# Early expert tiles with 512-column matmuls, their halves added on VectorE, their weight splits made on GpSimd

## The chip, the cores and the metric

One core of one Trainium2 chip runs the whole program. The metric is device time in microseconds (us): the median of the runs, lower is better. Engines: TensorE (PE; its weight loads are listed as PEld), VectorE (DVE), ScalarE (ACT), GpSimd (POOL) and SyncE (SP), which issues the DMAs.

## The reference

Two layers over 256 tokens of width 1024. Each layer has a mixer part (a combined input projection, three kinds of attention, gates, an output projection) and a PEER part, where the change lies:

```python
def peer_ffn(h, w_query, q_norm_peer, sub_keys_1, sub_keys_2, expert_u, expert_v):
    qr = rms_norm((h @ w_query).reshape(bsz, seq, PEER_HEADS, PEER_DKEY), q_norm_peer)
    s1 = jnp.einsum('bshd,hnd->bshn', qr[..., :half], sub_keys_1)
    s2 = jnp.einsum('bshd,hnd->bshn', qr[..., half:], sub_keys_2)
    v1, i1 = lax.top_k(s1, PEER_TOPK)
    v2, i2 = lax.top_k(s2, PEER_TOPK)
    ...
    top_s, top_pos = lax.top_k(cand_s, PEER_TOPK)
    idx = jnp.take_along_axis(cand_i, top_pos, axis=-1)
    g = jax.nn.softmax(top_s, axis=-1)
    ...
        u = jnp.take(expert_u, ix, axis=0)
        act = jax.nn.gelu(jnp.einsum('td,ted->te', hx, u))
        vv = jnp.take(expert_v, ix, axis=0)
        return jnp.einsum('te,ted->td', (gx * act), vv)
```

The kernel does not gather. It computes gelu(u . h) for all 16384 experts (128 tiles of 128 experts), multiplies by the routing weights, which are zero for experts not chosen, and multiplies by all of expert_v.

## The kernel before, in words

Weights come as a stream of tiles of 128x1024 fp32 through four raw buffers. ScalarE rounds each tile to fp32r (`head`, output `hi`, L496), and VectorE makes the rest raw - hi (`rest_of`, output `lo`, L873). Activations are kept in the same way as `mov_hi` and `mov_lo`, in 12 slots of 256 columns. A product is three matmuls: high weights by high activations, high weights by low activations, low weights by high activations (`product`, L1453 to L1455). A tile has 8 chunks (KC) of 128 rows, so an "up" tile is 24 matmuls of 256 columns into one of two PSUM banks `pj`. `hi` and `lo` have four buffers each (SPLIT): the head of tile t+3 waits until tile t-1 is done.

The 128 up tiles of a layer fall in two groups. The first 96 (EARLY) run while VectorE finds the top 16 keys of 8 heads for two blocks of tokens and turns positions into expert indices (the picks, L1315 to L1326). ScalarE applies gelu straight from the bank (`early_group`, L757) and frees the bank. VectorE's splits of these tiles are placed by hand between the top-k instructions (`split_early`). After tile 80 (EXP_AT) ScalarE changes its function table to take the softmax's exponents; after tile 84 (ROUTE_AT) TensorE transposes the indices and weights, and VectorE copies them (`route_in`). Then come 32 mixed tiles (STEPS): in each, TensorE also multiplies one-hot rows of 8 tokens (`tokens`, L1814), made by VectorE (`onehot_a`, L1351), by GpSimd (even groups of four tokens, `quad`, L484) and by ScalarE (odd ones, L788 and L792). The one-hots of GpSimd and ScalarE lie in slots 8 to 11 of `mov_hi` and `mov_lo`. Last come 128 down tiles with 512-column matmuls into `wk`.

Each engine runs its own program in order. Semaphores: `hi_done`, `lo_done` (splits made), `tile_done` (tile multiplied), `out_free` (bank read out), `hot_b` (one-hots made), `hot_used`. In the text tile 0 is the first early tile, tile 96 the first mixed one.

Of the kernel before, what the change touches and what calls it, by code (L numbers as in the profile page):

```python
# [20 lines left out]
P = 128  # L21
# [90 lines left out]
def trunk(nc, stream, par_dram, const_dram, mix_dram, taba_dram, keys_dram, front_dram, ada_dram, x_dram, out_dram):  # L112
# [4 lines left out]
    with ctx:  # L117
# [11 lines left out]
        mov_hi = sb("mov_hi", [P, 12, SEQ], f32r)  # L129
        mov_lo = sb("mov_lo", [P, 12, SEQ], f32r)  # L130
        w_hi = mov_hi[:, KC:KC + 4, :]
        w_lo = mov_lo[:, KC:KC + 4, :]
# [13 lines left out]
        onehot_b = [w.rearrange("p a b -> p (a b)").rearrange("p (r i) -> p r i", r=8) for w in (w_hi, w_lo)]  # L146
# [185 lines left out]
        route_in = sem("route_in")  # L332
        hot_a = sem("hot_a")
# [115 lines left out]
        def _(pool):  # L449
            for l in range(DEPTH):  # L450
# [39 lines left out]
        def _(act):  # L490
# [45 lines left out]
            for l in range(DEPTH):  # L536
# [324 lines left out]
        def _(dve):  # L861
# [80 lines left out]
            for l in range(DEPTH):  # L942
# [293 lines left out]
                early = [0]  # L1236

                def split_early(n):
                    for _ in range(min(n, EARLY - early[0])):
                        j = early[0]  # L1240
                        rest_of(L0 + (T_PEER + AHEAD + j), j + AHEAD)
                        early[0] += 1

                split_early(1)
# [9 lines left out]
                for u in range(17):  # L1254
# [15 lines left out]
                    split_early(1)  # L1270
# [6 lines left out]
                    split_early(1)  # L1277
# [4 lines left out]
                    split_early(u % 2)  # L1282
# [8 lines left out]
                    split_early(1)  # L1291
# [18 lines left out]
                split_early(1)  # L1310
                for n in range(2):
                    for b in range(2):
                        hot = pick.rearrange("p (c j) -> p c j", j=16)
                        pf = pos_f[:, n, b * 128:(b + 1) * 128]
                        one_hots = step(nc.vector.tensor_tensor(  # L1315
                            hot, pf.unsqueeze(2).to_broadcast([P, 128, 16]),
                            iota[:, 0:16].unsqueeze(1).to_broadcast([P, 128, 16]), ALU.is_equal))
                        split_early(2 if n + b else 1)
                        dve.wait_ge(dve_step, one_hots)
                        hot4 = pick.rearrange("p (u k j) -> p u k j", u=8, k=16)  # L1320
                        picked = step(nc.vector.tensor_tensor(
                            hot4, hot4, sel_if[:, b * 8:b * 8 + 8, n, :].unsqueeze(2).to_broadcast([P, 8, 16, 16]),
                            ALU.mult))
                        split_early(1)
                        dve.wait_ge(dve_step, picked)
                        link(nc.vector.tensor_reduce(idx_tok[:, n, b * 128:(b + 1) * 128], hot, AX.X, ALU.add))  # L1326
                        split_early(2 if n and b else 1)
                assert early[0] <= EXP_AT
                split_early(EXP_AT - early[0])
# [3 lines left out]
                split_early(1)  # L1333
# [5 lines left out]
                split_early(ROUTE_AT - early[0])  # L1339
# [110 lines left out]
        def _(pe):  # L1450
# [28 lines left out]
            for l in range(DEPTH):  # L1479
# [299 lines left out]

                def early_tile(j, between=None):  # L1780

                    project(L0 + (T_PEER + j), j, O_PEER + j, (j + 1) % 2, None if j else M_2, between=between,
                            between_at=KC - 1).then_inc(tile_done, 1)
# [5 lines left out]
                with pe.Fori(1, ROUTE_AT // 4) as i:  # L1789
                    for j in range(4):  # L1790
                        project(L0 + i * 4 + (T_PEER + j), j, i * 4 + (O_PEER + j), (j + 1) % 2).then_inc(tile_done, 1)
# [7 lines left out]
                for j in range(EARLY - ROUTE_AT):  # L1799
                    project(L0 + (T_PEER + ROUTE_AT + j), j, O_PEER + ROUTE_AT + j, (j + 1) % 2).then_inc(tile_done, 1)  # L1800
# [177 lines left out]
```

## Time and profile before

| | us |
|---|---|
| median of 3 runs | 2183.56 (2183.55 to 2184.15) |
| profiled execution, its span | 2181.1 |
| early tiles of the first layer | about 327 to 603 |
| mixed tiles of the first layer | about 603 to 752 |
| down tiles of the first layer | about 752 to 1097 |
| the same three in the second layer | about 1401 to 2171 |

The span runs from the first to the last instruction of the profiled execution. What is outside of it, and the difference between this execution and the median, make 2.5 us together. Busy times of the matmul rows overlap each other (a matmul is recorded as 283 ns while the next starts 120 ns later), so the rate has to be read from starts or from counts in a stretch.

### The profile page before, as it was taken

What the parts mean: (1) busy time and instruction counts of PE and PEld (TensorE: products, weight loads), DVE (VectorE), ACT (ScalarE), POOL (GpSimd) and SP (SyncE); (2) the same over time, 40 slices, a digit from 0 to 9 for tenths busy, and PEclk for the clock granted to TensorE, in tenths of its full rate; (3) what the DMA queues carried; (4) which work ended last, traced back from release to release, by engine and by line L of the source; (5) the groups of instructions that cost most, each with busy time, mean ns of one, the idle gap of its engine ahead of it and who ended that gap; (6) DMA issues with size and microseconds to landing.
All of it is one profiled execution on the core that took longest, in us unless ns stands there. A gap on an engine that the chain in (4) does not pass through costs nothing.

```text
span 2181.1 us, 43026 instructions
## 1 busy us (share of the span) xinstructions
PE 2151.9 (99%) x15008; PEld 1989.8 (91%) x15008; DVE 1680.4 (77%) x3258; ACT 1233.9 (57%) x2168; POOL 245.7 (11%) x298
## 2 busy tenths in 40 slices
PE   6999999999999999999999999999999999999999
PEld 5889999999999988888888899999999999888887
DVE  8777777889499956777577878788886997567765
ACT  5656575444577655555566565644455776555554
POOL 0210000000166400000002100000002662000000
PEclk8999999999999999999999999999999999999999
DMA  9466655555533367787665666455555334687864
GB/s 352 156 223 229 204 188 173 182 182 182 184 122 110 125 193 260 258 253 231 192 202 176 221 231 206 162 183 183 179 177 175 115 116 144 200 272 258 254 211 171
DMA packets 115440, 427.29 MB, mean 196 GB/s; under 512 B 12816, under 2 KB 13072, under 8 KB 113680
## 3 DMA queue, kind: packets, MB, share of 16 engines
q1 hardware_dynamic: 115344, 426.08, 58.2%
q8 instruction: 51, 0.84, 0.2%
q14 instruction: 45, 0.37, 0.0%
HBM read 424.99 MB, written 1.05 MB: 195 GB/s over the span
## 4 chain that ended last, share of the span: by engine, by line
PE 96%; DVE 2%; ACT 1%; DMA 1%; issue 0%; SPq 0%; ACTq 0%; DVEq 0%
PE pj L1453 18%; PE pj L1455 18%; PE pj L1454 18%; PE wk L1453 11%; PE wk L1455 11%; PE wk L1454 11%; PE wk L1814 5%; PE wk L1583 1%; PE wk L1560 1%; DMA arena<-in_front 1%; PE wk L1576 1%; PE wk L1522 1%; DVE arena L878 0%; PE wk L1743 0%; ACT hi L496 0%
## 5 line engine op out<-in xcount | busy, mean ns | idle before, releaser
L873 DVE TENSOR_TENSOR lo<-raw,hi 128x1024 fp32r<-128x1024 f32 x683 | 843.3, 1236 | 417.7 <-ACT hi L496 412.1
L496 ACT ACTIVATE hi<-raw 128x1024 fp32r<-128x1024 f32 x683 | 721.4, 1057 | 470.9 <-PE wk L1455 341.5
L1453 PE MATMUL pj<-mov_hi,hi 128*128 128x256 f32 x3008 | 867.8, 288 | 1.8 <-DVE x L1204 1.3
L1455 PE MATMUL pj<-mov_hi,lo 128*128 128x256 f32 x3008 | 851.5, 283 | 0.0
L1454 PE MATMUL pj<-mov_lo,hi 128*128 128x256 f32 x3008 | 850.9, 283 | 0.0
L1453 PEld LDWEIGHTS pj<-mov_hi,hi 128*128 128x128 f32 x3008 | 577.0, 192 | 10.9 <-issue 8.3
L1454 PEld LDWEIGHTS pj<-mov_lo,hi 128*128 128x128 f32 x3008 | 576.5, 192 | 0.1
L1455 PEld LDWEIGHTS pj<-mov_hi,lo 128*128 128x128 f32 x3008 | 575.9, 191 | 0.0
L1453 PE MATMUL wk<-hi,mov_hi 128*128 128x512 f32 x1024 | 398.5, 389 | 0.0
L1454 PE MATMUL wk<-lo,mov_hi 128*128 128x512 f32 x1024 | 398.4, 389 | 0.0
L1455 PE MATMUL wk<-hi,mov_lo 128*128 128x512 f32 x1024 | 398.4, 389 | 0.0
L484 POOL TENSOR_SCALAR mov_hi<-const,routes 128x128 fp32r<-128x128 f32 x256 | 199.4, 795 | 1012.8 <-DVE gateT L1343 866.7
L757 ACT ACTIVATE arena<-pj 128x256 f32 (+1 forms) x192 | 73.9, 385 | 275.4 <-PE pj L1455 275.4
L1455 PEld LDWEIGHTS wk<-hi,mov_lo 128*128 128x128 f32 x1024 | 192.2, 188 | 40.1
L1454 PEld LDWEIGHTS wk<-lo,mov_hi 128*128 128x128 f32 x1024 | 192.2, 188 | 39.9
L1453 PEld LDWEIGHTS wk<-hi,mov_hi 128*128 128x128 f32 x1024 | 192.2, 188 | 39.6
L1351 DVE TENSOR_SCALAR onehot_a<-const,routes,gateT 128x128 f32<-128x128 f32 x512 | 148.4, 352 | 2.2 <-PE wk L1814 2.2
L878 DVE SCALAR_TENSOR_TENSOR arena<-arena,silu_c 128x1024 f32<-128x1024 f32 x87 | 105.9, 1225 | 11.4 <-DMA arena<-in_ada 11.0
L1395 DVE TENSOR_TENSOR mov_lo<-arena,mov_hi 128x256 fp32r<-128x256 f32 x256 | 106.9, 418 | 0.0
L827 ACT ACTIVATE mov_hi<-arena 128x256 fp32r (+1 forms) x256 | 101.8, 399 | 2.8 <-DVE arena L1360 2.8
L788 ACT ACTIVATE mov_lo<-const,routes 128x128 fp32r<-128x128 f32 x256 | 81.0, 397 | 0.0
L1453 PE MATMUL pj<-u,hi 128*128 128x258 f32 x240 | 70.3, 293 | 3.2 <-DVE u L905 2.0
(207 smaller groups left out, 1896.1 us busy)
## 6 DMA issues: line engine op xcount, KB each, us to landing
raw<-in_stream SPq DMA_DIRECT2D x684, 512.0 KB, 3.4
arena<-in_ada SPq DMA_DIRECT2D x72, 512.0 KB, 4.8
onehot_a<-in_ada SPq DMA_DIRECT2D x24, 512.0 KB, 4.3
arena<-in_front SPq DMA_DIRECT2D x8, 1024.0 KB, 14.8
arena<-in_taba SPq DMA_DIRECT2D x2, 1536.0 KB, 8.7
arena<-in_keys SPq DMA_DIRECT2D x2, 1024.0 KB, 5.5
x<-in_xT SPq DMA_DIRECT2D x1, 1024.0 KB, 14.8
arena<-in_mix SPq DMA_DIRECT2D x2, 512.0 KB, 4.2
```

The source lines that it names most:

```text
L484: e = nc.gpsimd.tensor_scalar(onehot_b[0][:, quad % 4 * 2 + r, :], iota, idx2T[:, t:t + 1], None, ALU.is_equal)
L496: nc.scalar.activation(hi[j % SPLIT][:, :], raw[j % RAW][:, :], ACT.Copy).then_inc(hi_done, 1)
L788: e = nc.scalar.activation(onehot_b[1][:, slot + r, :], iota, ACT.Abs, bias=idx2T[:, quad * 4 + r:quad * 4 + r + 1], scale=-1.0)
L827: nc.scalar.activation(w_hi[:, s, :], group_of(n), ACT.Copy).then_inc(w_head, 1)
L873: nc.vector.tensor_tensor(lo[j % SPLIT][:, :], raw[j % RAW][:, :], hi[j % SPLIT][:, :].bitcast(f32), ALU.subtract).then_inc(lo_done, 1)
L878: nc.vector.scalar_tensor_tensor(tile, tile, 1.0, silu_c[:, :], ALU.mult, ALU.mult, accum_out=col)\
L1351: e = nc.vector.tensor_scalar(onehot_a[:, quad % 2 * 4 + r, :], iota, idx1T[:, t:t + 1], gateT[:, t:t + 1], ALU.is_equal, ALU.mult)
L1395: nc.vector.tensor_tensor(w_lo[:, s, :], group_of(n), w_hi[:, s, :].bitcast(f32), ALU.subtract).then_inc(w_rest, 1)
L1453: pe.matmul(out, w_h, m_h, start=first, stop=False)
L1454: pe.matmul(out, w_h, m_l, start=False, stop=False)
L1455: return pe.matmul(out, w_l, m_h, start=False, stop=last)
L1814: last = pe.matmul(wk[:, 2 + quad % 4, :].rearrange("p (i t) -> p t i", t=4)[:, r, :], onehot_a[:, quad % 2 * 4 + r, :], onehot_b[half][:, ...
```

## The change

For the 96 early tiles the activations' high and low parts now lie side by side (`mov`, high at 0, low at 1), so that one matmul of 512 columns multiplies the high weights by both; the low weights by the high activations stay a matmul of 256 columns. The bank then holds two halves. VectorE adds them into `arena` (`meets`) and frees the bank; ScalarE applies gelu in place in `arena`. GpSimd makes `lo` for these 96 tiles in a loop ahead of its one-hots. The picks are cut into 16 pieces of 4 units where there were 8 steps of 8 units.

```diff
-        mov_hi = sb("mov_hi", [P, 12, SEQ], f32r)
-        mov_lo = sb("mov_lo", [P, 12, SEQ], f32r)
+        mov = sb("mov", [P, KC + 4, 2, SEQ], f32r)
+        mov_hi, mov_lo = mov[:, :, 0, :], mov[:, :, 1, :]
...
+                T0 = l * TILES + T_PEER + AHEAD
+                wait_alone(pool, lo_done, T0)
+                with pool.Fori(0, EARLY // 4) as i:
+                    for j in range(4):
+                        wait_alone(pool, hi_done, i * 4 + (T0 + j + 1))
+                        s = (j + AHEAD) % SPLIT
+                        nc.gpsimd.tensor_tensor(lo[s][:, :], raw[s][:, :], hi[s][:, :].bitcast(f32),
+                                                ALU.subtract).then_inc(lo_done, 1)
                 wait_alone(pool, route_in, 6 * l + 6)
                 for quad in range(0, QUADS, 2):
...
-                    act.wait_ge(tile_done, t + 1 + SPLIT)
-                    nc.scalar.activation(arena[:, bass.ds(i * 4 + j, 1), :].squeeze(1), pj[(j + 1) % 2][:, 0:SEQ],
-                                         ACT.Gelu_apprx_tanh).then_inc(out_free, 1)
+                    act.wait_ge(out_free, i * 4 + (l * OUTS + O_PEER + j + 1 + 2))
+                    group = arena[:, bass.ds(i * 4 + j, 1), :].squeeze(1)
+                    nc.scalar.activation(group, group, ACT.Gelu_apprx_tanh).then_inc(gelu_done, 1)
...
+                def meets(count):
+                    for _ in range(min(count, EARLY - met[0])):
+                        n = met[0]
+                        dve.wait_ge(tile_done, L0 + (T_PEER + n + 1 + SPLIT))
+                        halves = pj[(n + 1) % 2]
+                        nc.vector.tensor_reduce(arena[:, n, :], halves[:, :].rearrange("p (h s) -> p s h", h=2), AX.X,
+                                                ALU.add).then_inc(out_free, 1)
+                        met[0] += 1
...
+                    for k in range(KC):
+                        w_h, w_l = chunk(j, k)
+                        both = mov[:, k, :, :].rearrange("p h s -> p (h s)")
+                        if k == KC - 1:
+                            pe.matmul(out[:, 0:SEQ], w_l, mov_hi[:, k, :], start=False, stop=False)
+                            last = pe.matmul(out[:, :], w_h, both, start=False, stop=True)
+                        else:
+                            pe.matmul(out[:, :], w_h, both, start=k == 0, stop=False)
+                            pe.matmul(out[:, 0:SEQ], w_l, mov_hi[:, k, :], start=False, stop=False)
```

TensorE, the start of an early tile in the loop, before:

```order
L1453 MATMUL pj<-mov_hi,hi 128x256 [waits out_free,lo_done]
L1454 MATMUL pj<-mov_lo,hi 128x256
L1455 MATMUL pj<-mov_hi,lo 128x256
L1453 MATMUL pj<-mov_hi,hi 128x256
L1454 MATMUL pj<-mov_lo,hi 128x256
```

and the same place now, with two matmuls where there were three:

```order
L1806 MATMUL pj<-mov,hi 128x512 [waits out_free,lo_done]
L1807 MATMUL pj<-mov,lo 128x256
L1806 MATMUL pj<-mov,hi 128x512
L1807 MATMUL pj<-mov,lo 128x256
L1806 MATMUL pj<-mov,hi 128x512
```

GpSimd, what stands ahead of the mixed tiles, before (the last attention product, then the one-hots):

```order
L467 TENSOR_TENSOR arena<-arena,small 128x2x256
L484 TENSOR_SCALAR mov_hi<-const,routes 128x128 [waits route_in]
L484 TENSOR_SCALAR mov_hi<-const,routes 128x128 x7
L484 TENSOR_SCALAR mov_hi<-const,routes 128x128 [waits hot_used]
L484 TENSOR_SCALAR mov_hi<-const,routes 128x128 x3
```

and now, where the loop (one turn of it is shown, 24 turns run) comes before the one-hots (L494), so that these can't start until tile 98 is split:

```order
L468 TENSOR_TENSOR arena<-arena,small 128x2x256
L481 UNCONDITIONAL_BRANCH [waits lo_done]
L481 ISA
L485 TENSOR_TENSOR lo<-raw,hi 128x1024 [waits hi_done]
L355 REGISTER_ALU
L485 TENSOR_TENSOR lo<-raw,hi 128x1024 [waits hi_done]
L355 REGISTER_ALU
L485 TENSOR_TENSOR lo<-raw,hi 128x1024 [waits hi_done]
L355 REGISTER_ALU
L485 TENSOR_TENSOR lo<-raw,hi 128x1024 [waits hi_done]
L494 ISA [waits route_in]
L494 TENSOR_SCALAR mov<-const,routes 128x128 x8
```

VectorE, the change from early to mixed tiles, before:

```order
L873 TENSOR_TENSOR lo<-raw,hi 128x1024 [waits hi_done] x8
L1351 TENSOR_SCALAR onehot_a<-const,routes,gateT 128x128 [waits route_in]
L1351 TENSOR_SCALAR onehot_a<-const,routes,gateT 128x128 x3
L873 TENSOR_TENSOR lo<-raw,hi 128x1024 [waits hi_done] x2
L1351 TENSOR_SCALAR onehot_a<-const,routes,gateT 128x128 x4
L873 TENSOR_TENSOR lo<-raw,hi 128x1024 [waits hi_done] x2
```

and now, with the sum of a tile that is done in the place of each split of a tile that is three ahead:

```order
L1253 TENSOR_REDUCE arena<-pj 128x256 [waits tile_done] x8
L1359 TENSOR_SCALAR onehot_a<-const,routes,gateT 128x128 [waits route_in]
L1359 TENSOR_SCALAR onehot_a<-const,routes,gateT 128x128 x3
L1253 TENSOR_REDUCE arena<-pj 128x256 [waits tile_done] x2
L1359 TENSOR_SCALAR onehot_a<-const,routes,gateT 128x128 x4
L1253 TENSOR_REDUCE arena<-pj 128x256 [waits tile_done] x2
```

## Rows read from the trace of the kernel before

**Rows 1.** The page: TensorE's busy time, and the chain's shares by engine.

```profile
PE 2151.9 (99%) x15008; PEld 1989.8 (91%) x15008; DVE 1680.4 (77%) x3258; ACT 1233.9 (57%) x2168; POOL 245.7 (11%) x298
PE 96%; DVE 2%; ACT 1%; DMA 1%; issue 0%; SPq 0%; ACTq 0%; DVEq 0%
```

**Rows 2.** Stretches: length, busy PE, PEld, DVE, ACT, POOL (instructions), clock, DMA, GB/s.

```profile
342.00:558.00 216.00, 216.00 (x1803) 216.00 (x1802) 185.47 (x469) 102.74 (x152) 0.00 (x0) 1.00 0.54 182
605.00:740.00 135.00, 135.00 (x1163) 135.00 (x1162) 133.38 (x316) 100.06 (x260) 90.06 (x117) 1.00 0.35 116
760.00:1090.00 330.00, 330.00 (x1458) 273.25 (x1457) 217.48 (x299) 166.09 (x243) 0.00 (x0) 1.00 0.72 232
```

**Rows 3.** ScalarE's timeline in the early tiles: start, length, instruction, [idle before].

```profile
342.63 0.39 ACT L757 ACTIVATE arena<-pj 128x256 f32 x1 [1.56 <-PE pj L1455]
...
345.51 0.39 ACT L757 ACTIVATE arena<-pj 128x256 f32 x1 [1.54 <-PE pj L1455]
```

**Rows 4.** GpSimd's instructions by line and shape: busy us, mean ns, idle before.

```profile
L484 POOL TENSOR_SCALAR mov_hi<-const,routes 128x128 fp32r<-128x128 f32 x256 | 199.4, 795 | 1012.8 <-DVE gateT L1343 866.7 <-PE wk L1814 146.2
L458 POOL TENSOR_TENSOR arena<-arena 128x1024 f32<-128x1024 f32 x4 | 7.6, 1892 | 83.9 <-ACT arena L582 83.9
```

**Rows 5.** GpSimd and VectorE side by side: timelines at 83 to 95 and at 569 us.

```profile
90.27 2.40 POOL L467 TENSOR_TENSOR arena<-arena,small 128x256 f32<-128x256 f32 x2 [5.61 <-DVE small L1028]
91.12 1.02 DVE L1017 COPY arena<-wk 128x384 f32<-128x384 f32 x2
92.64 1.89 POOL L458 TENSOR_TENSOR arena<-arena 128x1024 f32<-128x1024 f32 x1
93.32 2.29 DVE L873 TENSOR_TENSOR lo<-raw,hi 128x1024 fp32r<-128x1024 f32 x1 [1.18 <-ACT hi L496]
569.31 1.25 DVE L873 TENSOR_TENSOR lo<-raw,hi 128x1024 fp32r<-128x1024 f32 x1 [0.22 <-ACT hi L496]
```

**Rows 6.** GpSimd's one-hots (L484): shortest, median and longest in ns.

```profile
L484 POOL TENSOR_SCALAR mov_hi<-const,routes x256: 595/602/1652, 569.3 to 1815.7; 128x128 fp32r<-128x128 f32 x128
```

**Rows 7.** VectorE and GpSimd timelines: VectorE's one-hots alone, then beside GpSimd's.

```profile
591.12 1.11 DVE L1351 TENSOR_SCALAR onehot_a<-const,routes,gateT 128x128 f32<-128x128 f32 x4
...
603.87 1.17 DVE L1351 TENSOR_SCALAR onehot_a<-const,routes,gateT 128x128 f32<-128x128 f32 x4 [1.09 <-PE wk L1814]
603.97 3.26 POOL L484 TENSOR_SCALAR mov_hi<-const,routes 128x128 fp32r<-128x128 f32 x4 [28.23 <-PE wk L1814]
```

**Rows 8.** VectorE by line: a 128x512 read of `pj`, a pick product, a pick sum.

```profile
L1171 DVE TENSOR_TENSOR arena<-pj,arena 128x512 f32<-128x512 f32 x16 | 11.0, 689 | 2.6 <-PE pj L1455 2.3
L1315 DVE TENSOR_TENSOR arena<-arena,const 128x2048 f32<-128x2048 f32 x8 | 18.3, 2285 | 0.0
L1326 DVE TENSOR_REDUCE arena<-arena 128x128 f32<-128x2048 f32 x8 | 18.2, 2280 | 0.0
```

**Rows 9.** VectorE's timeline in the top-k: the blocks between splits.

```profile
353.77 0.09 DVE L1280 MATCH_VALUE_LOAD arena<-arena 128x8 f32 x1
...
355.80 1.21 DVE L873 TENSOR_TENSOR lo<-raw,hi 128x1024 fp32r<-128x1024 f32 x1
356.93 0.09 DVE L1295 MATCH_VALUE_LOAD arena<-arena 128x8 f32 x1
...
358.57 1.21 DVE L873 TENSOR_TENSOR lo<-raw,hi 128x1024 fp32r<-128x1024 f32 x1
```

**Rows 10.** ScalarE's timeline at the softmax (tiles 79 to 83).

```profile
555.75 0.39 ACT L757 ACTIVATE arena<-pj 128x256 f32 x1 [1.55 <-PE pj L1455]
...
560.19 1.06 ACT L496 ACTIVATE hi<-raw 128x1024 fp32r<-128x1024 f32 x1
```

**Rows 11.** ScalarE's timeline at the end of the early tiles, and TensorE's first one-hot product.

```profile
597.43 1.27 ACT L788 ACTIVATE mov_lo<-const,routes 128x128 fp32r<-128x128 f32 x4
...
599.26 1.05 ACT L496 ACTIVATE hi<-raw 128x1024 fp32r<-128x1024 f32 x1
...
602.71 1.05 PE L1814 MATMUL wk<-mov_hi,onehot_a 128*128 128x128 f32 x8
```

More of the change, by code:

```diff
@@ L1234, in _ @@
                 query_scaled(N_QUERY - 1)
[L1236 to L1244, printed above, removed]
+                met = [0]
+                def meets(count):
[6 more added lines that the diff above has]
+                        met[0] += 1
                 def step(ins):
@@ L1309, in _ @@
                 link(nc.vector.tensor_copy(pos_f, pos_i))
-                split_early(1)
+                meets(1)
                 for n in range(2):
-                    for b in range(2):
-                        hot = pick.rearrange("p (c j) -> p c j", j=16)
-                        pf = pos_f[:, n, b * 128:(b + 1) * 128]
+                    for u in range(0, 16, 4):
+                        at = slice(u * TOPK, (u + 4) * TOPK)
+                        hot = pick[:, 0:4 * TOPK * 16].rearrange("p (c j) -> p c j", j=16)
                         one_hots = step(nc.vector.tensor_tensor(
-                            hot, pf.unsqueeze(2).to_broadcast([P, 128, 16]),
-                            iota[:, 0:16].unsqueeze(1).to_broadcast([P, 128, 16]), ALU.is_equal))
-                        split_early(2 if n + b else 1)
+                            hot, pos_f[:, n, at].unsqueeze(2).to_broadcast([P, 4 * TOPK, 16]),
+                            iota[:, 0:16].unsqueeze(1).to_broadcast([P, 4 * TOPK, 16]), ALU.is_equal))
+                        meets(1)
                         dve.wait_ge(dve_step, one_hots)
-                        hot4 = pick.rearrange("p (u k j) -> p u k j", u=8, k=16)
+                        hot4 = pick[:, 0:4 * TOPK * 16].rearrange("p (u k j) -> p u k j", u=4, k=16)
                         picked = step(nc.vector.tensor_tensor(
-                            hot4, hot4, sel_if[:, b * 8:b * 8 + 8, n, :].unsqueeze(2).to_broadcast([P, 8, 16, 16]),
-                            ALU.mult))
-                        split_early(1)
+                            hot4, hot4, sel_if[:, u:u + 4, n, :].unsqueeze(2).to_broadcast([P, 4, 16, 16]), ALU.mult))
+                        meets(1)
                         dve.wait_ge(dve_step, picked)
[L1326 to L1329, printed above, removed]
+                        link(nc.vector.tensor_reduce(idx_tok[:, n, at], hot, AX.X, ALU.add))
+                assert met[0] <= EXP_AT, met
+                meets(EXP_AT - met[0])
                 dve.wait_ge(q_rr, l + 1)
@@ L1778, in turn_sums, with project_wide @@
                                      ident).then_inc(q_turned, 1)
+                def project_wide(t, j, o, chunks=None, between=None):
+                    out = pj[(j + 1) % 2]
+                    pe.wait_ge(lo_done, t + 1)
+                    pe.wait_ge(out_free, l * OUTS + o + 1)
+                    for k in range(KC):
+                        if chunks is not None:
+                            pe.wait_ge(mov_ready, l * M_READY + (chunks + k + 1))
+                        if between is not None and k == KC - 1:
+                            between()
+                        w_h, w_l = chunk(j, k)
[6 more added lines that the diff above has]
+                            pe.matmul(out[:, 0:SEQ], w_l, mov_hi[:, k, :], start=False, stop=False)
+                    last.then_inc(tile_done, 1)
                 def early_tile(j, between=None):
-                    project(L0 + (T_PEER + j), j, O_PEER + j, (j + 1) % 2, None if j else M_2, between=between,
-                            between_at=KC - 1).then_inc(tile_done, 1)
+                    project_wide(L0 + (T_PEER + j), j, O_PEER + j, None if j else M_2, between)
                 early_tile(0, last_scores)
```

32 lines of the change are left out of this document (17 added, 15 removed).

## The prediction

> **What bounds the kernel now.** I read the page first: TensorE is busy for 99% of the span and carries 96% of the chain that ended last [rows 1]. So only TensorE's time, or a new wait of TensorE, moves the result. Next come the stretches. Early tiles: 1803 matmuls in 216.0 us, 119.8 ns each; down tiles: 1458 matmuls of 512 columns in 330.0 us, 226.3 ns each [rows 2]. TensorE is busy through all three stretches and the granted clock is 1.00 in each. ScalarE's gelus of two successive early tiles start 2.88 us apart, which is 24 x 0.12 [rows 3]. VectorE is busy 185 of 216 us in the early tiles and 133 of 135 in the mixed ones; GpSimd does nothing in the early tiles and 90 of 135 in the mixed ones [rows 2].
>
> **TensorE's gain.** Doubling the columns adds 226.3 - 119.8 = 106.5 ns, so 13.3 ns of each matmul do not depend on its columns. The change streams as many columns in 16 matmuls per tile as before in 24, and saves this part 8 times. A tile becomes 8 x (0.2263 + 0.1198) = 2.77 us in place of 2.88: 0.11 less. For 96 tiles and 2 layers that is 20 to 21 us; I take **20.7**. That a short matmul can follow a long one at the same cost isn't seen in the trace; from both sides, a tile costs between 16 x 0.1198 + 8 x 0.1065 (the same 2.77, nothing extra) and the old 2.88 (gain nil).
>
> **GpSimd's split.** No row shows GpSimd subtracting into fp32r. The nearest in shape is the product of two 128x1024 tiles, 1.89 us [rows 4]; the nearest in output type are the one-hots into fp32r, 602 ns at the median for only 128 elements [rows 6]. If all of that went by the element, 1024 would take 4.8 us. I take 1.89, because operation kind, shape and operand count match, and the one-hot also reads its key from a column and compares. 1.89 fits in 2.77; anything above 2.77 makes GpSimd the bound. The Trainium skill (GPSIMD Engine Reference, section Elementwise side-by-side cycle accounting) gives 4497 ns for a two-input operation of 2048 fp32, so an estimate of some 2.3 us for 1024; the row of 1.89 for the same shape disagrees.
>
> **The way to a bank and to the next split.** VectorE's sum reads 128x512 from `pj`: 0.69 by the row of another operation of this size [rows 8]. ScalarE's gelu, which freed the bank, now waits for it, and its next head waits behind the gelu. From the end of tile t-1: sum 0.7, gelu 0.4, head 1.05, split 1.9, with handoffs some 4.2 us; the split is tile t+3's, wanted 3 x 2.77 = 8.3 us on. So 4 us spare. The bank is tighter: the sum must be over within the next tile, so VectorE may come late by 2.77 - 0.69 - 0.2 = 1.9 us.
>
> In the top-k the blocks between sums are at most 2.03 us (353.77 to 355.80) and 1.64 us (356.93 to 358.57) [rows 9]; with 0.65 for the sum, 2.7 and 2.3 against 2.77. No stall, and VectorE does less than before (0.65 in place of 1.13 a tile). The raw buffers are freed about a microsecond later with most of two tiles to spare. The finer cut of the picks does the same elements in twice the instructions; it costs nothing while VectorE stays within its 1.9 us.
>
> **GpSimd and VectorE side by side.** At 92.64 GpSimd runs 1.89 us; VectorE's split, begun at 93.32, takes 2.29 where it takes 1.25 otherwise, so it sat out the other's end. Copies out of PSUM beside another GpSimd operation go undisturbed, two in 1.02 [rows 5]. The other way round, a one-hot that begins with a split takes 1652 ns and not 602: 1.05 lost [rows 5, 6]. VectorE's one-input one-hots are hardly touched: four take 1.17 beside GpSimd and 1.11 alone [rows 7]. So VectorE operations with two SBUF inputs and GpSimd's exclude each other, and others don't. [...]
>
> In the top-k there is one such operation in three tiles (the add), which waits at most 1.9 in a block of 1.64: 3.5 + 0.65 against 2.77 is 1.4 late, inside 1.9. The picks are different. A piece has two operations of 1024 elements (half of 2285 ns [rows 8]) to two tiles, each taking turns with a split: 2 x (1.89 + 1.05) = 5.9 us against 5.54 for two tiles. VectorE falls back 0.36 us in each of 8 pieces, about 2.9, of which 1.9 are spare: **1.0 us per layer**. Bounds: 0, if turns interleave, and 2.5, if an operation holds the other off for 1.15 rather than 1.05.
>
> **Softmax.** From tile 79's gelu to head 83 it is 4.44 us, two table loads among them, and the head ends at 561.25, 5.5 after the tile [rows 10]. Now 0.75 later (the sum), then the split 1.9 and a handoff: 8.3 after tile 79. Tile 83 starts at 3 x 2.77 = 8.3. I count **0.1 per layer**, at most 0.5.
>
> **The first mixed tile.** This is the cost. GpSimd's first one-hots were ready some 30 us early (idle 28.23 after them [rows 7]). Now they stand behind the split of tile 98. Count from the end of tile 94, when TensorE has 2.77 us left. ScalarE's own one-hots (597.43 to 599.26, 1.83 [rows 11]) stand between the gelu of tile 93 and head 97. Gelu 93 ends at -2.77 + 0.75 + 0.35 = -1.67, the one-hots at 0.15, head 97 at 1.2, gelu 94 at 1.5, head 98 at 2.55. GpSimd: split 97 from 1.25 to 3.15, split 98 to 5.1. Then four one-hots: one begun alone and three more, 0.6 x 4 = 2.4 [rows 6]; with handoffs TensorE's first one-hot product starts at 7.6. It would have started at 2.77: **4.8 us per layer**, between 4 and 5.5. The mixed stage behind it starts with the same supplies relative to that moment (VectorE's third one-hots wait for that product before and after), so its 149 us stay.
>
> **Sum.** -20.7 + 2 x (4.8 + 1.0 + 0.1) = -8.9. The profiled execution, 2181.1, becomes 2172.2; with the 2.5 us that lie between it and the median, **2174.7 us**, -0.4%. A measurement here tells about 0.2% (4.4 us) from no change.
>
> **The rivals.**
> The split is slower than the product of rows 4, at around 2.3 us. TensorE still isn't held in the top-k, but a pair of turns is 3.35, a piece 6.7 against 5.54: 9.3 late, less 1.9 spare, 7.4 per layer. The first mixed tile loses 0.4 for each of splits 97 and 98, 5.6, the softmax 0.5. Together 27 against 20.7: about 2190. It ends on the other side; it decides from a split of about 2.15 us. For it: different operands and a conversion. Against: the 1.89. Chance 14%. The estimate from the GPSIMD page above is this case.
> GpSimd is the bound: a split over 2.77, say 3.4 (of the one-hot's 0.6 a guessed 0.2 fixed, 0.4 for 128 elements, times 8). A tile then goes by 3.4, 0.52 more than before: 96 x 2 x 0.52 = 100, and 2 x 8 at the handoff and picks: about 2300. For it: rows 6. 
> The change does not do what it says: long and short matmuls in turn go no faster, tile 2.88. Then the stalls remain alone: 2183.6 + 11.5 = 2195. Chance 4%.
> The handoff costs less, or the mixed stage makes up for it, since VectorE and GpSimd there come with less behind them: down to 2166. Against it: TensorE has no idle time there to give back. Chance 8%.
> Small waits that I don't see (twice as much at the picks, a wait in each turn of the loop) take 5 us more: 2180. Chance 7%.
>
> **How the numbers follow.** My forecast (2171 to 2178) has the remaining 54%. Faster by over 0.2% (below 2179.2): forecast, the smaller handoff and a third of the small waits, 64%. Within 0.2%: the rest of the small waits and the lower end of the slow split, up to 2188, 12%. Slower: 24%. The range takes in the smaller handoff below and the split of 2.3 above, 2166 to 2191, and leaves out the GpSimd bound, the exclusion in the top-k and the unchanged tile.
>
> **What the profile after would show.** 512- and 256-column matmuls in turn starting 0.226 and 0.120 apart; gelus 2.77 apart; GpSimd's splits at 1.9 where alone; VectorE's sums at 0.69; idle time of TensorE of 5 us ahead of the first one-hot product, released by GpSimd, and about 1 us late in the picks, released by a sum. I am wrong if the splits are longer than 2.15, if a sum takes over 1 us (strided reads), or if ScalarE, which now waits for VectorE and not for TensorE, lets a late sum run on into late heads.

## The result and the profile after

The changed kernel takes 2210.36 us (median of 4 runs, 2208.34 to 2210.72) against 2183.56 for the kernel before on the same chip: ratio 1.0121, 95% interval 1.0108 to 1.0133, so slower by 1.2%. The profiled execution has a span of 2206.6 us, 25.5 more than before.

The page of the kernel after: the span, the busy times, and the chain that ended last, by engine.

```profile
span 2206.6 us, 40608 instructions
PE 2153.9 (98%) x13472; PEld 1912.3 (87%) x13472; DVE 1632.3 (74%) x3282; ACT 1240.3 (56%) x2168; POOL 731.4 (33%) x490
...
PE 88%; DVE 7%; ACT 1%; POOL 1%; issue 1%; DMA 1%; SPq 0%; ACTq 0%; POOLq 0%; DVEq 0%
```

TensorE has the 1,536 matmuls less that were promised, but its share of the chain fell from 96% [rows 1] to 88%, and VectorE's rose from 2 to 7%. TensorE's busy row gives no warning: at 2153.9 it is 2 us above that of before. The chain and the waits have to be read.

The kernel after, TensorE's waits: engine, its line, who was waited for, us in total, times, longest.

```profile
PE wk L1843 <- POOL mov L494: 11.8, 2, 6.0
PE pj L1806 <- POOL lo L485: 8.2, 27, 0.6
...
PE pj L1806 <- DVE arena L1253: 2.3, 2, 1.2
```

The first line is the handoff to the mixed tiles, once per layer. The second is new: 27 times an early tile waited for GpSimd's split, 25 times in the picks and once per layer, for 0.6 us, at the softmax. The last line is the end of the top-k, once per layer.

The kernel after, GpSimd's splits (shortest, median, longest in ns), then VectorE by line and shape (busy us, mean ns, idle before).

```profile
L485 POOL TENSOR_TENSOR lo<-raw,hi x192: 2347/2405/3442, 325.2 to 1694.4; 128x1024 fp32r<-128x1024 f32 x192
```

```profile
L1253 DVE TENSOR_REDUCE arena<-pj 128x256 f32<-128x512 f32 x192 | 132.3, 689 | 167.5 <-PE pj L1804 164.3
L1331 DVE TENSOR_TENSOR arena<-arena 128x1024 f32<-128x1024 f32 x16 | 41.9, 2621 | 0.0
L1325 DVE TENSOR_TENSOR arena<-arena,const 128x1024 f32<-128x1024 f32 x16 | 23.9, 1495 | 0.5
...
L1335 DVE TENSOR_REDUCE arena<-arena 128x64 f32<-128x1024 f32 x16 | 19.3, 1203 | 0.0
```

A split takes 2.40 us and not 1.89. The sum of halves takes 0.69, as in [rows 8]. Of the VectorE operations shown, those with two SBUF inputs grew (a product of 1024 elements is 1.22 alone and 2.62 here), and the TENSOR_REDUCE of the picks did not.

The picks in the kernel after, VectorE's timeline and then GpSimd's (start, length, instruction, count, [idle before]).

```profile
487.90 1.59 DVE L1325 TENSOR_TENSOR arena<-arena,const 128x1024 f32<-128x1024 f32 x1
489.42 0.68 DVE L1253 TENSOR_REDUCE arena<-pj 128x256 f32<-128x512 f32 x1
490.02 2.82 DVE L1331 TENSOR_TENSOR arena<-arena 128x1024 f32<-128x1024 f32 x1
492.76 0.68 DVE L1253 TENSOR_REDUCE arena<-pj 128x256 f32<-128x512 f32 x1
```

```profile
478.31 23.48 POOL L485 TENSOR_TENSOR lo<-raw,hi 128x1024 fp32r<-128x1024 f32 x7 [3.67 <-ACT hi L506]
```

Seven splits fill 23.48 us without a gap, 3.35 each: GpSimd is never idle, and each split loses about a microsecond to a VectorE operation as that loses time to it. The sums come 3.34 us apart (489.42 to 492.76). In these tiles GpSimd sets the pace.

The handoff in the kernel after: GpSimd's timeline, then TensorE's, then stretches (length; busy PE, PEld, DVE, ACT, POOL; granted clock, DMA, GB/s).

```profile
605.35 4.68 POOL L485 TENSOR_TENSOR lo<-raw,hi 128x1024 fp32r<-128x1024 f32 x2 [0.53 <-ACT hi L506]
610.10 4.67 POOL L494 TENSOR_SCALAR mov<-const,routes 128x128 fp32r<-128x128 f32 x8
```

```profile
606.23 0.40 PE L1804 MATMUL pj<-mov,hi 128*128 128x512 f32 x1
612.59 2.04 PE L1843 MATMUL wk<-mov,onehot_a 128*128 128x128 f32 x8 [5.96 <-POOL mov L494]
```

```profile
612.50:614.50 2.00, 1.91 (x9) 1.94 (x10) 0.00 (x0) 0.00 (x0) 2.00 (x4) 0.50 0.22 86
...
616.60:625.00 8.40, 8.40 (x75) 8.40 (x74) 6.99 (x18) 4.64 (x11) 5.34 (x8) 1.00 0.39 125
```

TensorE's first one-hot product starts at 612.59, 9.9 us later than the 602.71 of [rows 11]. After an idle time of 5.96 us the granted clock is 0.50, its lower level of 1.2 GHz, so that eight short matmuls take 2.04 us where they took 1.05. The second layer has the same with 5.80 us of idle time. The clock rows give what this costs: both times the clock stays down for 6.8 us. It falls 2.6 us into the first idle time and 4.6 into the second, so that 3.5 and 5.7 us of half clock lie behind the restart, and half of that is lost (1.7 and 2.7 us in the row of the mixed tiles below).

The stages by the starts of their first matmuls (worked out from both traces, us, first and second layer):

| stage | before | after |
|---|---|---|
| from the scores to the transposes after tile 83 | 241.5, 241.4 | 245.0, 245.0 |
| from there to the first one-hot product | 35.2, 35.2 | 40.7, 40.6 |
| mixed tiles | 148.9, 148.9 | 150.6, 151.6 |
| down tiles, to the first matmul behind them | 348.8, 348.8 | 348.8, 348.8 |

Some 3.0 us of the 25.5 lie in parts that the change leaves alone: 0.8 at the start, 1.7 in the second layer's mixers and 0.5 behind the last result.

### The profile page after: what moved, and what is told of

Same layout as the page of the kernel before. It is cut to its first block, busy times and chain, and to the rows that moved or that the text cites. A ratio compares the mean times of both kernels' runs of the same rounds, so it can differ in the third digit from the quotient of the medians.

```text
span 2206.6 us, 40608 instructions
## 1 busy us (share of the span) xinstructions
PE 2153.9 (98%) x13472; PEld 1912.3 (87%) x13472; DVE 1632.3 (74%) x3282; ACT 1240.3 (56%) x2168; POOL 731.4 (33%) x490
## 3 DMA queue, kind: packets, MB, share of 16 engines
HBM read 424.99 MB, written 1.05 MB: 193 GB/s over the span
## 4 chain that ended last, share of the span: by engine, by line
PE 88%; DVE 7%; ACT 1%; POOL 1%; issue 1%; DMA 1%; SPq 0%; ACTq 0%; POOLq 0%; DVEq 0%
PE pj L1806 11%; PE wk L1465 10%; PE wk L1463 10%; PE wk L1464 10%; PE pj L1463 10%; PE pj L1465 9%; PE pj L1464 9%; PE pj L1807 5%; PE wk L1843 5%; PE pj L1804 2%; DVE arena L1331 1%; DVE arena L1253 1%; DVE arena L1325 1%; POOL lo L485 1%; PE wk L1593 1%
## 5 line engine op out<-in xcount | busy, mean ns | idle before, releaser
L883 DVE TENSOR_TENSOR lo<-raw,hi 128x1024 fp32r<-128x1024 f32 x491 | 609.4, 1242 | 308.2 <-ACT hi L506 302.9
L485 POOL TENSOR_TENSOR lo<-raw,hi 128x1024 fp32r<-128x1024 f32 x192 | 488.3, 2556 | 458.6 <-ACT hi L506 458.6
L1806 PE MATMUL pj<-mov,hi 128*128 128x512 f32 x1344 | 484.6, 399 | 10.8 <-POOL lo L485 8.2
L1463 PE MATMUL pj<-mov,hi 128*128 128x256 f32 x1472 | 433.6, 295 | 1.4 <-DVE x L1214 1.3
L1465 PE MATMUL pj<-mov,lo 128*128 128x256 f32 x1472 | 417.6, 284 | 0.0
L1464 PE MATMUL pj<-mov,hi 128*128 128x256 f32 x1472 | 417.1, 283 | 0.0
L1463 PE MATMUL wk<-hi,mov 128*128 128x512 f32 x1024 | 398.5, 389 | 0.0
L1465 PE MATMUL wk<-hi,mov 128*128 128x512 f32 x1024 | 398.4, 389 | 0.0
L1464 PE MATMUL wk<-lo,mov 128*128 128x512 f32 x1024 | 398.3, 389 | 0.0
L1807 PE MATMUL pj<-mov,lo 128*128 128x256 f32 x1344 | 376.9, 280 | 0.0
L1806 PEld LDWEIGHTS pj<-mov,hi 128*128 128x128 f32 x1344 | 252.7, 188 | 73.0 <-issue 12.8
L1463 PEld LDWEIGHTS pj<-mov,hi 128*128 128x128 f32 x1472 | 283.1, 192 | 9.5 <-issue 7.1
L1464 PEld LDWEIGHTS pj<-mov,hi 128*128 128x128 f32 x1472 | 282.7, 192 | 0.1
L1465 PEld LDWEIGHTS pj<-mov,lo 128*128 128x128 f32 x1472 | 282.0, 192 | 0.0
L1807 PEld LDWEIGHTS pj<-mov,lo 128*128 128x128 f32 x1344 | 253.9, 189 | 7.0
L494 POOL TENSOR_SCALAR mov<-const,routes 128x128 fp32r<-128x128 f32 x256 | 196.7, 785 | 91.5 <-PE wk L1843 90.9
L1465 PEld LDWEIGHTS wk<-hi,mov 128*128 128x128 f32 x1024 | 192.3, 188 | 39.7
L1463 PEld LDWEIGHTS wk<-hi,mov 128*128 128x128 f32 x1024 | 192.3, 188 | 39.7
```

The lines of the kernel that those rows point to most:

```text
L485: nc.gpsimd.tensor_tensor(lo[s][:, :], raw[s][:, :], hi[s][:, :].bitcast(f32), ALU.subtract).then_inc(lo_done, 1)
L494: e = nc.gpsimd.tensor_scalar(onehot_b[0][:, quad % 4 * 2 + r, :], iota, idx2T[:, t:t + 1], None, ALU.is_equal)
L883: nc.vector.tensor_tensor(lo[j % SPLIT][:, :], raw[j % RAW][:, :], hi[j % SPLIT][:, :].bitcast(f32), ALU.subtract).then_inc(lo_done, 1)
L1463: pe.matmul(out, w_h, m_h, start=first, stop=False)
L1464: pe.matmul(out, w_h, m_l, start=False, stop=False)
L1465: return pe.matmul(out, w_l, m_h, start=False, stop=last)
```

## The experiments

The ratio of each is to the kernel before. Each expectation names its own theories A and B.

**The price of a split by itself.** Behind its own work, the kernel before times GpSimd operations one by one, three of each:

```diff
+            for _ in range(3):
+                alone(nc.gpsimd.tensor_tensor(raw[3][:, :], raw[0][:, :], raw[0][:, :], ALU.mult))
+            for _ in range(3):
+                alone(nc.gpsimd.tensor_tensor(raw[3][:, :], raw[0][:, :], raw[1][:, :], ALU.mult))
...
+            for _ in range(3):
+                alone(nc.gpsimd.tensor_tensor(l0, raw[0][:, :], h0.bitcast(f32), ALU.subtract))
+            for _ in range(3):
+                alone(nc.gpsimd.tensor_tensor(l0, raw[0][:, :], raw[0][:, :], ALU.mult))
```

> The kernel before, with GpSimd operations added behind its last work, each alone, three times: products and differences of 128x1024 with one or two different operands, into fp32 or fp32r, and one-hots. The changed kernel's split took 2.41 us at the median where the product of a tile by itself took 1.89. Theory A (two different operands cost more): the product of two different tiles into fp32 takes 2.3 to 2.4, and the same operand twice into fp32r 1.9. Theory B (the fp32r output costs more): the difference of two tiles into fp32 takes 1.9, into fp32r 2.4, and the same operand twice into fp32r 2.4 too. Theory C (subtract costs more than multiply): the product of two tiles 1.9, their difference 2.4. If the cost goes by the element, 512 elements take about 1.2 us in the slow form; if it is fixed, about 1.5.

Its timeline of GpSimd, one row of each kind: a product of a tile with itself; of two tiles; a difference of two tiles; the split as the change makes it; a product of a tile with itself into fp32r; half a split; a one-hot into fp32r (into f32 it takes the same).

```profile
2181.47 1.89 POOL L502 TENSOR_TENSOR raw<-raw 128x1024 f32<-128x1024 f32 x1 [0.18 <-POOL raw L502]
2188.13 2.34 POOL L504 TENSOR_TENSOR raw<-raw 128x1024 f32<-128x1024 f32 x1 [0.18 <-POOL raw L504]
2195.68 2.34 POOL L506 TENSOR_TENSOR raw<-raw 128x1024 f32<-128x1024 f32 x1 [0.18 <-POOL raw L506]
2210.79 2.34 POOL L510 TENSOR_TENSOR lo<-raw,hi 128x1024 fp32r<-128x1024 f32 x1 [0.18 <-POOL lo L510]
2217.90 1.89 POOL L512 TENSOR_TENSOR lo<-raw 128x1024 fp32r<-128x1024 f32 x1 [0.18 <-POOL lo L512]
2223.48 1.26 POOL L514 TENSOR_TENSOR lo<-raw,hi 128x512 fp32r<-128x512 f32 x1 [0.18 <-POOL lo L514]
2229.60 0.60 POOL L518 TENSOR_SCALAR lo<-const,routes 128x128 fp32r<-128x128 f32 x1 [0.20 <-POOL lo L518]
```

Neither the operation nor the fp32r output costs anything; a second, different operand costs 0.45 us. The row that the prediction priced the split by [rows 4] is the square of one tile (`projT` by `projT`).

**The wide matmuls of a tile first, then the narrow ones.** TensorE's tile in the top-k was 2.82 us after the change, not 2.77.

```diff
-                        if k == KC - 1:
-                            pe.matmul(out[:, 0:SEQ], w_l, mov_hi[:, k, :], start=False, stop=False)
-                            last = pe.matmul(out[:, :], w_h, both, start=False, stop=True)
-                        else:
-                            pe.matmul(out[:, :], w_h, both, start=k == 0, stop=False)
-                            pe.matmul(out[:, 0:SEQ], w_l, mov_hi[:, k, :], start=False, stop=False)
+                        pe.matmul(out[:, :], chunk(j, k)[0], both, start=k == 0, stop=False)
+                    for k in range(KC):
+                        last = pe.matmul(out[:, 0:SEQ], chunk(j, k)[1], mov_hi[:, k, :], start=False, stop=k == KC - 1)
```

> The changed kernel, with an early tile's eight 512-column matmuls first and its eight 256-column ones behind them, where they stood in turn. In turn a pair takes 0.352 us (tile 2.82) and not the 0.346 of the two rows of before. Theory A (taking turns between lengths costs some 6 ns a pair): the tile takes 2.77 us, and where TensorE is not held (52 tiles of the top-k and some 25 later ones per layer) the time falls by 0.05 x 77 x 2 = 8 us, to about 2203. Theory B (the pair costs this much in any order, because a 512-column matmul with fp32r activations read across two slots is slower): no change, 2210. In the picks GpSimd and VectorE hold the tiles at 3.3 us with either.

2208.74 us, ratio 1.0114 (1.0098 to 1.0131). Its VectorE timeline where nothing holds TensorE up:

```profile
580.09 0.69 DVE L1253 TENSOR_REDUCE arena<-pj 128x256 f32<-128x512 f32 x1 [2.10 <-PE pj L1803]
582.89 0.69 DVE L1253 TENSOR_REDUCE arena<-pj 128x256 f32<-128x512 f32 x1 [2.10 <-PE pj L1803]
```

A tile is 2.79 us, between the two theories: of the missing 0.05, 0.03 go to taking long and short matmuls in turn. Some 150 unhindered tiles should give 4.6 us, and the median moved by 1.6. From the scores to the transposes only 0.8 us are won in each layer, and 0.65 us go to a wait of TensorE for ScalarE in the first early tile that the kernel after hasn't. The profiled run also has a stretch at half the granted clock in the second layer's mixers (3.4 us from 1212.7), so the total alone decides nothing.

**VectorE makes the last 28 early splits.** GpSimd splits the first 68 tiles and comes early to its one-hots.

```diff
+POOL_N = 68
-                with pool.Fori(0, EARLY // 4) as i:
+                with pool.Fori(0, POOL_N // 4) as i:
...
+                        if n >= POOL_N:
+                            if n == POOL_N:
+                                dve.wait_ge(lo_done, L0 + (T_PEER + AHEAD + n))
+                            rest_of(L0 + (T_PEER + AHEAD + n), n + AHEAD)
```

> The changed kernel, with GpSimd making the splits of 68 early tiles only (through the picks) and VectorE those of the last 28 behind its sums, so that GpSimd is free for its one-hots early. Theory A (the loss ahead of the mixed tiles is GpSimd's late one-hots, and the loss at the start of the mixed stage is TensorE's clock after that idle time): the 6.0 us of idle time, the 1.6 and 2.6 us of a longer mixed stage and 0.8 us at the softmax go, in each layer; about 2192. Theory B (the mixed stage is longer because of the new layout of the activations or one-hots): the idle time goes but the mixed stage stays at 150.6 and 151.5 us; about 2196. The picks keep their 3.3 us tiles in both.

2194.52 us, ratio 1.0051 (1.0034 to 1.0068). From the transposes to the first one-hot product it now takes 34.4 us for 40.7, and the mixed tiles 148.9. The picks' tiles stay at 3.3. So a GpSimd that is free from tile 68 on is worth 15.8 us. The time lies between A's 2192 and B's 2196; the mixed tiles, back at 148.9, decide for A. Its profiled run has 2.8 us more than the kernel after in the second layer's mixers, with a half clock there too (see the last experiment).

**VectorE makes all splits, TensorE as changed** (POOL_N = 0, GpSimd's loop removed).

> The changed kernel, with all early splits on VectorE, each behind a sum, and none on GpSimd: the 512-column matmuls and the sums alone. Theory A (VectorE is then the bound): in the top-k three tiles need 4.55 us of search, 3 sums of 0.62 and 3 splits of 1.13, 9.8 us against 8.46: 1.3 more in each of 17 steps, 22 us per layer; in the picks 2 tiles need 7.0 against 5.64: 11 us per layer; less 5.8 per layer for the shorter tiles: about 2235. Theory B (what the changed kernel lost came with GpSimd's port, and VectorE has room): under 2190.

2232.54 us, ratio 1.0222 (1.0205 to 1.0239). A tile in the top-k is 3.24 us, VectorE sets its pace, and TensorE waits for sums, as A had it:

```profile
PE pj L1802 <- DVE arena L1245: 38.5, 72, 1.1
```

So GpSimd's splits, dear as they are, save 22 us over leaving them on VectorE. Its timeline also gives what the end of the top-k costs with no split beside it; under it the same two instructions in the kernel after:

```profile
489.93 0.18 DVE L1308 COPY arena<-arena 128x16 f32<-128x16 f32 x1
...
490.60 0.29 DVE L1312 TENSOR_SCALAR arena<-arena 128x256 uint32<-128x256 uint32 x1
```

```profile
471.01 0.86 DVE L1312 COPY arena<-arena 128x16 f32<-128x16 f32 x1
...
472.37 2.43 DVE L1316 TENSOR_SCALAR arena<-arena 128x256 uint32<-128x256 uint32 x1
```

**A split at the price the prediction took.** GpSimd reads the same tile twice; the low weights are then zero, and their product is missing from the result.

```diff
-                        nc.gpsimd.tensor_tensor(lo[s][:, :], raw[s][:, :], hi[s][:, :].bitcast(f32),
+                        nc.gpsimd.tensor_tensor(lo[s][:, :], raw[s][:, :], raw[s][:, :],
```

> The changed kernel, with GpSimd's split reading the raw tile twice (raw - raw) instead of raw and hi: the early tiles' low weights are then zero, which leaves one of the three products out of the result, but the operation costs 1.89 us as the row of before did, and not 2.34 to 2.41. Theory A (the price of the split was the step that failed; the sum of the prediction holds otherwise): tiles of 2.82, 1 us per layer at the picks, 4.8 and the 1.7 of a lower clock ahead of the mixed tiles: 2183.6 - 11.5 + 2 x 7.7 = 2187 to 2190. Theory B (most of the picks' loss and of the rest does not come from the split's length): 2200 or more.

2192.91 us, ratio 1.0045 (1.0029 to 1.0062). GpSimd's splits, then the picks on VectorE, then TensorE's wait at the handoff:

```profile
L485 POOL TENSOR_TENSOR lo<-raw x192: 1889/1896/2873, 325.0 to 1677.9; 128x1024 fp32r<-128x1024 f32 x192
```

```profile
487.40 1.23 DVE L1325 TENSOR_TENSOR arena<-arena,const 128x1024 f32<-128x1024 f32 x1
488.55 0.68 DVE L1253 TENSOR_REDUCE arena<-pj 128x256 f32<-128x512 f32 x1
489.15 2.31 DVE L1331 TENSOR_TENSOR arena<-arena 128x1024 f32<-128x1024 f32 x1
491.39 0.68 DVE L1253 TENSOR_REDUCE arena<-pj 128x256 f32<-128x512 f32 x1
```

```profile
PE wk L1843 <- POOL mov L494: 9.5, 2, 4.8
```

This is the kernel that the prediction described. Two tiles of the picks take 5.8 us (2.84 between the sums shown, 2.98 for the tile before; 5.9 was worked out), sixteen take 0.8 to 0.9 us more than at 2.82 (1.0 was worked out), and the handoff leaves TensorE idle for 4.8 and 4.7 (4.8). And yet it is 18.2 us over 2174.7. The price of the split therefore explains 17.5 us of the miss, and half of it is left to others. A had 2187 to 2190 here and is short by 3.

**The picks spread over 28 tiles**, with GpSimd making all splits: each piece of the picks gets one or two sums more.

```diff
+                        meets(1 + u // 4 % 2)
```

> The changed kernel, with the eight pieces of the picks spread over the 28 tiles up to the softmax (a sum or two also behind each piece's own sum) in place of 16 tiles with 12 more behind them. GpSimd still makes all splits. Theory A (the picks lose because two operations with two SBUF operands and two splits do not fit in two tiles): 28 splits of 2.35 and 16 turns of 1.05 are 82.6 us against 28 x 2.82 = 79.0, and the split is 3.5 us early, so the 8.5 us per layer of the picks fall to 1 or less: about 2194. Theory B (each meeting costs TensorE by itself, since VectorE's sum is late and the bank not free): the 16 turns cost about as much as before, 2206 or more.

2201.72 us, ratio 1.0084 (1.0067 to 1.0101): 8.6 us won, between A's 16 and B's 4 at most. The stage up to the transposes gains 4.0 us in each layer and not 7.5. The 28 tiles of the picks now take 2.8 to 3.5, 2.90 on average, and the four tiles at the softmax 0.6 more than in the kernel after: turns with VectorE are still paid, and a split of 2.40 leaves only 0.42 in a tile of 2.82 to make up for them.

**Picks spread, and VectorE splits from tile 48 on** (the line above with POOL_N = 48), so that GpSimd has no split beside the picks, nor before its one-hots.

> The spread picks, and GpSimd makes the splits of the first 48 early tiles only; VectorE makes the other 48, behind its sums. GpSimd and VectorE then hardly meet, and GpSimd's one-hots are early. VectorE in the picks: 8 pieces of 3.4 us and 28 tiles of 1.75, 76.4 us against 79.0. Theory A (nothing but the port, the late one-hots and the clock behind them cost time): tiles of 2.82 throughout, 2183.6 - 11.5 and some 2 us per layer at the softmax and at the end of the top-k: 2173 to 2177. Theory B (VectorE, busy 97%, comes late for a bank every few tiles): 2180 to 2190.

2177.60 us (7 runs), ratio 0.9971 (0.9959 to 0.9982): 0.3% faster than before, 32.8 us below the changed kernel, just above A's 2173 to 2177. Against the spread picks with all splits on GpSimd, 24.1 us are won. Its VectorE timeline in the picks:

```profile
504.04 1.22 DVE L1330 TENSOR_TENSOR arena<-arena,const 128x1024 f32<-128x1024 f32 x1
505.18 0.68 DVE L1254 TENSOR_REDUCE arena<-pj 128x256 f32<-128x512 f32 x1
505.78 1.21 DVE L884 TENSOR_TENSOR lo<-raw,hi 128x1024 fp32r<-128x1024 f32 x1
506.91 1.22 DVE L1336 TENSOR_TENSOR arena<-arena 128x1024 f32<-128x1024 f32 x1
```

Every operation is back at its time alone.

**The same with the wide matmuls first.**

> As the kernel with spread picks and 48 tiles split by VectorE, with the 512-column matmuls of a tile first and the 256-column ones behind them, which made a tile 2.79 us and not 2.82. Theory A (TensorE is now the bound in all early tiles): 0.03 x 96 x 2 = 6 us less than that kernel, 2167 to 2171. Theory B (VectorE is the bound in the picks): 3 us less or nothing.

2174.08 us (5 runs, 2172.41 to 2176.25), ratio 0.9961 (0.9947 to 0.9975), 3.5 below the one before it, between A's 6 and B's 3. It is the best of all. The page's chain and two stretches:

```profile
PE 95%; DVE 2%; ACT 1%; DMA 1%; issue 0%; SPq 0%; ACTq 0%; DVEq 0%
```

```profile
345.00:560.00 215.00, 214.28 (x1227) 188.22 (x1225) 189.49 (x503) 109.04 (x156) 101.73 (x43) 1.00 0.55 184
605.00:740.00 135.00, 135.00 (x1163) 135.00 (x1162) 133.96 (x320) 100.82 (x263) 88.33 (x115) 1.00 0.34 113
```

**Idle time alone.** What pulls the clock down at the handoff? In the kernel before, with no split on GpSimd, only its first one-hots are held back; in a second kernel the four further ones are left out.

```diff
                 wait_alone(pool, route_in, 6 * l + 6)
+                wait_alone(pool, tile_done, l * TILES + (T_PEER + EARLY + SPLIT))
+                for n in range(4):
+                    nc.gpsimd.tensor_scalar(onehot_b[0][:, 0, :], iota, idx2T[:, 0:1], None,
+                                            ALU.is_equal).then_inc(probed, 1)
+                    wait_alone(pool, probed, l * 4 + n + 1)
```

> The kernel before, with GpSimd's first one-hots held back until tile 95 is multiplied and four further one-hots of 0.80 us each ahead of them, in each layer. TensorE should then sit idle for 0.1 + 4 x 0.8 + 4 x 0.6, about 5.8 us, ahead of its first one-hot product, with GpSimd making no split at all. Theory A (the idle time alone brings the fall of the granted clock to half that the changed kernel shows behind it): a half-clock stretch of about 6.8 us from some 3 us into the idle time, and a mixed stage of 150.6 to 151.6 us in place of 148.9, so that the span grows by 2 x (5.8 + 2.2) = 16 us. Theory B (the half clock comes from something else in the changed kernel): the clock stays at 1.00, the mixed stage at 148.9, the span grows by 11.6 us.

> The same without the four further one-hots: TensorE idle for about 0.1 + 4 x 0.6 = 2.5 us ahead of the first one-hot product. If a shorter idle time does not cost the clock, the clock stays at 1.00, the mixed stage at 148.9, and the span grows by 2 x 2.5 = 5 us; if it does, by about 2 us more per layer, 9 us. Both theories of the other run allow either; it bounds what a smaller handoff loss would be worth.

One time each: 2200.86 and 2191.03 us beside 2184.0. The first, TensorE's timeline and the stretch behind it; then the same of the second.

```profile
609.74 2.04 PE L1820 MATMUL wk<-mov_hi,onehot_a 128*128 128x128 f32 x8 [5.91 <-POOL mov_hi L490]
```

```profile
609.70:615.60 5.90, 5.86 (x27) 5.89 (x28) 2.31 (x5) 0.00 (x0) 5.46 (x8) 0.50 0.07 12
```

```profile
607.00 1.13 PE L1815 MATMUL wk<-mov_hi,onehot_a 128*128 128x128 f32 x8 [2.71 <-POOL mov_hi L485]
```

```profile
607.00:615.00 8.00, 8.00 (x69) 8.00 (x70) 6.45 (x14) 3.47 (x10) 7.40 (x11) 1.00 0.29 101
```

Idle for 5.9 us, the clock falls to half and the mixed tiles take 151.8 and 151.5 us; idle for 2.7, it stays, and they take 149.0. Theory A is right: in the kernel before, with no split on GpSimd, the idle time alone does it, and costs 2.6 to 2.9 us per layer beyond itself. Beside the kernel before on the same chip the first grew by 16.9 us (16 expected), the second by 7.0 (5 expected, or 9 with a fall of the clock). Of the second span's growth of 8.1 over the [rows 1] execution 5.9 are in the handoffs and the mixed tiles, the rest outside of the early and mixed tiles.

The length of the idle time doesn't decide by itself. In the second layer's mixers TensorE stood idle for 2.2 to 2.4 us in five of the kernels above. In four of them (wide matmuls first, last 28 splits on VectorE, all splits on VectorE, picks spread) a half clock of 3.4 us followed, in the fifth (first 48 splits on GpSimd) none. TensorE's timeline and the stretch behind it in the kernel with the last 28 splits on VectorE:

```profile
1206.12 0.85 PE L1591 MATMUL wk<-const,arena 128*128 128x128 f32 x6 [2.37 <-issue]
```

```profile
1207.05:1210.45 3.40, 3.40 (x19) 3.40 (x18) 1.88 (x5) 1.06 (x2) 1.88 (x3) 0.50 0.54 194
```

and in the kernel whose first 48 splits are on GpSimd:

```profile
1198.22 0.52 PE L1592 MATMUL wk<-const,arena 128*128 128x128 f32 x3 [2.26 <-issue]
```

```profile
1198.20:1202.00 3.80, 3.78 (x32) 3.67 (x34) 2.35 (x6) 1.46 (x3) 2.28 (x4) 1.00 0.70 264
```

## Why the prediction was wrong, step by step

**The step that failed is "I take 1.89, because operation kind, shape and operand count match".** The operand count didn't match: that row squares one tile. The split of two tiles takes 2.34 alone and 2.40 in place. What it set off is the prediction's own first rival, "a pair of turns is 3.35, a piece 6.7": the picks' tiles are 3.35 apart, and sixteen tiles take 52.0 us for 45.1 at 2.82, a loss of 6.9 per layer (7.4 worked out). 2.4 lies above the rival's 2.15 from which it decides. That rival was put at about 2190 and is still 20 us short, so the price of the split is not the only step that failed. The estimate from the Trainium skill (GPSIMD Engine Reference, section Elementwise side-by-side cycle accounting) of some 2.3 us was right, and was overruled by a row of another case. With the split at 1.89 the kernel was 17.5 us faster; that is this step's share of the 35.7 us between forecast and result.

**TensorE's gain, "a tile becomes 2.77": right in kind, mis-sized.** Nothing in the trace showed a short matmul behind a long one. The prediction said so and took the better bound. Measured: 2.82, and 2.79 with all long ones first. 0.05 x 192 = 9.6 us, nearly half of the 20.7.

**"Its 149 us stay": wrong.** 150.6 and 151.6. The supplies were as before; the clock wasn't. An idle time of 4.8 us, as predicted, is enough: in the kernel with the cheap split the mixed tiles take 151.6 and 151.5. In the kernel after it is 4.3 us for both layers.

**The first mixed tile: the mechanism right.** 4.8 predicted and 4.8 measured with a split of 1.89. In the kernel after it is 5.96, of which the price of two splits is 0.9 of the 1.2 more.

**"VectorE's one-input one-hots are hardly touched": wrong, by a misreading of [rows 7].** VectorE had begun there at 603.87 and GpSimd at 603.97, and it was GpSimd that paid: 3.26 us for four one-hots of 0.6. Its rule that only VectorE operations with two SBUF inputs exclude GpSimd's doesn't hold: beside a split that has begun, VectorE's copy takes 0.86 for 0.18, a one-input `tensor_scalar` 2.43 for 0.29, and the one-hots 4.26 for 1.11:

```profile
595.81 4.26 DVE L1359 TENSOR_SCALAR onehot_a<-const,routes,gateT 128x128 f32<-128x128 f32 x4
```

The delayed one-hots themselves cost TensorE little (the three tiles from the sum at 595.21 to that at 603.88 take 8.7 us for 8.5). At the end of the top-k three tiles take 9.8 us for 8.5, which the prediction had at nothing; with the cheap split 8.8. The Trainium skill (SBUF - State Buffer, section Practical consequences) names copy, cast and `tensor_scalar` among the operations that can take the port pair that VectorE and GpSimd share. For the copy and the `tensor_scalar` the traces agree, with the numbers above.

**No stall in the top-k, the sums at 0.69, MAX8 and the like and the picks' TENSOR_REDUCE (1.20) undisturbed: right.** Of `tensor_reduce` the same section of the Trainium skill says that on this chip it never contends, and the 1.20 agrees.

**Softmax, "0.1 per layer": mis-sized.** The four tiles behind tile 79 take 12.1 us, 0.8 more than at 2.82 (ScalarE's head 83, then a split of 2.4). But before they took 12.0, 0.5 more than at 2.88, which the prediction didn't see; the change adds 0.3 to 0.4.

**The sum.** Over the predicted span of 2172.2 the measured one is 34.4 (by the medians 35.7; the profiled execution is the fastest of the four). The tile makes 9.6, the mixed tiles 4.3, the way from the transposes to the first one-hot product 2.8. Up to the transposes it is 15.0: the stage grew by 3.5 to 3.6 where 84 tiles at 0.06 less should have taken 5.0 from it, a loss of 8.6 per layer against 1.1, and the end of the top-k (1.4), the picks (6.9) and the softmax (0.3) make it up. The parts left alone are 3.0. Together 34.7, within the rounding of these stages. Of the 1.7 us in the second layer's mixers 1.0 is one idle time of TensorE (before 1212.29) that the trace of before hasn't; why it comes stays open. The 0.8 at the start is no more than these traces differ by anyway: the same stretch takes 326.0 to 327.5 us in them.

## What to carry to other kernels

Before a price is taken from a row of the same shape, look at which operands it reads: a tile with itself is another case than two tiles, and where a figure of the Trainium skill and a row disagree, that is a question to answer and not a vote. Where two engines exclude each other, work out which one has no slack: a helper engine that fills 2.4 of 2.8 us can't pay for a single turn, and its work belongs where its partner runs nothing that excludes it (here, with the picks spread, splits of the first 48 tiles were 24 us better than of all 96). And idle time of TensorE can have a second price behind it: here 4.7 to 6.0 us of it always brought a half clock, 2.7 at the same place didn't, and 2.2 to 2.4 elsewhere did four times in five. Only the clock in the trace tells.

## What the runs showed of the hardware

- GpSimd, 128x1024 f32: 1.89 us for a tile with itself, 2.34 for two tiles, whether product or difference, f32 or fp32r output; 128x512 of two tiles 1.26.
- TensorE, 256- and 512-column matmuls in turn: 2.82 us for eight of each; grouped 2.79; by [rows 2] 2.77.
- TensorE idle for 4.7 to 6.0 us ahead of the mixed tiles: granted clock 0.50 for 6.8 us in all, 1.7 to 2.9 us lost; idle for 2.7 there: none. Idle for 2.2 to 2.4 us in the second layer's mixers: granted clock 0.50 for 3.4 us in four traces, 1.00 in one.
- VectorE's one-input COPY and TENSOR_SCALAR, from SBUF to SBUF, wait out a GpSimd operation that has begun (0.86 for 0.18, 2.43 for 0.29); TENSOR_REDUCE does not (1.20 for 1024 elements beside GpSimd's splits).
